# Rope's turn on VectorE, 65-to-96-token experts as two items, and the first item begun on two numbers set ahead of the list

## What is computed

```python
def rope(t, pos):                       # on q and k of the 12 dilated heads, head size 64
    t1, t2 = t[..., :32], t[..., 32:]
    return concat([t1 * cos - t2 * sin, t2 * cos + t1 * sin], -1)

# each layer
h = LN(ALPHA * h + mixer(h))            # 12 dilated (roped) + 4 forgetting heads, then w_out
probs = softmax(h @ w_router + b)       # 16 experts in 4 groups
group = argmax over groups of the sum of the two best; experts = the 2 best inside it
for e in range(16):                     # a = silu(x @ w_gate[e]) * (x @ w_up[e]); y = a @ w_down[e]
    ...
h = LN(ALPHA * h + sum of gate * y)
```

## Time and profile before

| | us |
|---|---|
| median of 3 runs | 1326.74 (1326.23 to 1327.0) |
| profiled execution | 1324.69 |
| its span, first to last instruction | 1323.0 |
| TensorE matmuls busy in it | 1114.8 (84%) |
| VectorE busy | 314.2 (24%) |
| ScalarE busy | 182.2 (14%) |
| moved by DMA | 444.7 MB, mean 336 GB/s |

### The profile page before, as it was taken

How to read it: one execution, slowest core, us unless ns; L and a number is a source line. 1 busy time by engine, 2 the same in 40 slices (tenths; PEclk the granted TensorE clock), 3 DMA queues, 4 the chain that set the end, 5 groups by cost and what they waited for, 6 DMA issues and landing times.

```text
span 1323.0 us, 16816 instructions
## 1 busy us (share of the span) xinstructions
PE 1114.8 (84%) x6068; PEld 566.8 (43%) x6069; DVE 314.2 (24%) x797; ACT 182.2 (14%) x373; POOL 4.6 (0%) x12
## 2 busy tenths in 40 slices
PE   7999988899976779777999996999998876766585
PEld 5776543344432233323677653444453332232232
DVE  0544541111111111113255363001111111111123
ACT  2233310000010000010223330100101000001000
POOL 0000000000000000000000000000000000000000
PEclk9999988899998789889899998999999987887888
DMA  9913379999999999999931434776979999999994
GB/s 377 371 64 144 138 307 428 386 429 428 428 429 429 428 428 428 428 403 424 390 128 64 174 136 192 257 261 233 430 315 377 428 428 428 428 428 429 428 404 188
DMA packets 34713, 444.70 MB, mean 336 GB/s; under 512 B 4081, under 2 KB 4337, under 8 KB 5873
## 3 DMA queue, kind: packets, MB, share of 16 engines
q1 hardware_dynamic: 33520, 439.96, 80.4%
q0 software_dynamic: 1152, 4.19, 0.8%
HBM read 443.09 MB, written 1.05 MB: 336 GB/s over the span
## 4 chain that ended last, share of the span: by engine, by line
PE 56%; DMA 36%; issue 4%; DVE 3%; ACT 0%; DVEq 0%; ACTq 0%; SPq 0%
DMA ring<-in_w_down_dram 36%; PE lo L696 10%; PE lo L589 9%; PE acc L490 9%; PE lo L601 7%; PE acc L468 5%; PE lo L576 3%; PE acc L564 3%; PE acc L654 1%; PE lo L564 1%; PE acc L542 1%; PE lo L530 1%; PE acc L736 1%; PE lo L519 1%; PE acc L763 1%
## 5 line engine op out<-in xcount | busy, mean ns | idle before, releaser
L601 PE MATMUL lo<-ring,work 128*32 128x512 f32 x2112 | 275.6, 669 | 135.0 <-DMA ring<-in_w_down_dram 124.4
L601 PEld LDWEIGHTS lo<-ring,work 128*32 128x32 f32 x2112 | 68.2, 118 | 319.2 <-issue 158.0
L589 PE MATMUL lo<-ring,work 128*64 128x512 f32 x672 | 151.9, 608 | 18.7 <-issue 13.1
L576 PEld LDWEIGHTS lo<-work,h 128*128 128x128 f32 x1088 | 131.0, 194 | 57.1 <-issue 53.5
L576 PE MATMUL lo<-work,h 128*128 128x128 f32 x1088 | 147.4, 285 | 1.9 <-DVE work L1314 1.9
L696 PE MATMUL lo<-ring,work 128*128 128x512 f32 x288 | 127.0, 601 | 11.4 <-issue 11.4
L490 PE MATMUL acc<-ring 128*128 128x256 f32 x512 | 120.9, 392 | 0.0
L490 PEld LDWEIGHTS acc<-ring 128*128 128x128 f32 x512 | 99.4, 197 | 15.5 <-issue 1.6
L589 PEld LDWEIGHTS lo<-ring,work 128*64 128x64 f32 x672 | 49.1, 140 | 116.4 <-issue 109.4
L696 PEld LDWEIGHTS lo<-ring,work 128*128 128x128 f32 x288 | 55.2, 193 | 80.3 <-issue 80.3
L1034 ACT ACTIVATE work<-lo 64x512 f32<-64x512 f32 x22 | 13.1, 594 | 468.5 <-PE lo L601 468.5
(11 more groups left out here) (191 smaller groups left out, 679.8 us busy)
## 6 DMA issues: line engine op xcount, KB each, us to landing
ring<-in_w_gate_dram SPq DMA_DIRECT2D x64, 2048.0 KB, 14.9
ring<-in_w_up_dram SPq DMA_DIRECT2D x64, 2048.0 KB, 22.6
ring<-in_w_down_dram SPq DMA_DIRECT2D x64, 2048.0 KB, 21.9
ring<-in_w_in_dram SPq DMA_DIRECT2D x24, 1024.0 KB, 26.2
ring<-in_w_out_dram SPq DMA_DIRECT2D x8, 1024.0 KB, 28.8
ln_gb<-in_ln_dram POOLq DMA_DIRECT2D x8, 512.0 KB, 11.4
cst<-in_consts_dram SPq DMA_DIRECT2D x1, 1408.0 KB, 17.6
h<-in_x_dram SPq DMA_DIRECT2D x1, 1024.0 KB, 5.3
```

The source lines that it names most:

```text
L576: mm = nc.tensor.matmul(lo[:, 2 + k // 4, (k % 4) * P:(k % 4 + 1) * P], h[:, t, k * P:(k + 1) * P], place_t[:, t], start=(k % 4 == 0 and t ...
L589: mm = nc.tensor.matmul(lo[half * W:(half + 1) * W, bank, :], lhsT, ring[:, s, at:at + 512], start=start, stop=stop, skip_group_check=True)
L601: return nc.tensor.matmul(lo[at * T:(at + 1) * T, bank, :], lhsT, ring[:, s, col:col + 512], start=start, stop=stop, skip_group_check=True)
```

## The change

Three parts.

1. `rotate` and its matrix are gone. VectorE multiplies the 32-partition quarters of q and k with a signed sin, each read from its neighbour's quarter and written to its own place; then cos, then the sum. Two waits on the rotation and one on `roped` disappear; the release of two ring slots moves from `rotate(1)` and `rotate(5)` to the first matmul of the query/key product of pairs 2 and 6.
2. The kinds grow from 3 used to 7: an expert of 65 to 96 tokens becomes a narrow item (the first 64) and a tiny one (the rest); one of 97 to 128 stays one wide item. The list is computed in another way, for up to 23 items in place of 19.
3. VectorE sets `n` and the kind of the first item ahead of the list and raises `first_ready`; TensorE waits for that between the two halves of the first gather.

```diff
-MOST = NEXP + (2 * SEQ - 1) // (P + 1)
+LIMITS = (T, W, W + T, P, P + T, P + W)
+TINY_KINDS, NARROW_KINDS, FIRST_TINY, KINDS = 3, 5, 2, 7
+FIRST_KIND = (2, 0, 1, 0, 0, 0)
+SECOND_KIND = (0, -2, 2, -1, 2, 3)
+SECONDS = (0, 1, -1, 1, 0, 0)
+MOST = NEXP + 2 * SEQ // (W + 1)
...
-                    if p < PAIRS_DIL:
-                        rotate(l, p, {1: ring_free[V_SLOT[0][1]], 5: ring_free[V_SLOT[1][1]]}.get(p))
...
-                gather(range(KB))
-                pe.wait_ge(plan_ready, l + 2)
+                gather(first_half)
+                pe.wait_ge(first_ready, l + 1)
                 n = pe.value_load(n_i[0:1, bass.ds(l, 1)], min_val=NEXP, max_val=MOST)
+                gather(second_half)
                 with pe.Fori(0, n) as j:
...
+                    pe.wait_ge(plan_ready, l + 2)
+                    pe.sem_inc(passed, 1)
...
                 v.wait_ge(qk_copied, PAIRS * l + p + 1)
-                nc.vector.tensor_tensor(dst, raw, cos, ALU.mult)
-                v.wait_ge(rot_done, PAIRS_DIL * l + p + 1)
-                step(nc.vector.tensor_tensor(part, rot, sin, ALU.mult))
-                nc.vector.tensor_tensor(dst, dst, part, ALU.add).then_inc(roped, 1)
+                for q in range(4):
+                    to, at = slice(32 * q, 32 * q + 32), slice(32 * (q ^ 1), 32 * (q ^ 1) + 32)
+                    nc.vector.tensor_tensor(turned_part[to], raw[at], sin[at], ALU.mult)
+                step(nc.vector.tensor_tensor(dst, raw, cos, ALU.mult))
+                nc.vector.tensor_tensor(dst, dst, turned_part, ALU.add).then_inc(roped, 1)
...
+                step(nc.vector.tensor_tensor(weighed, over.unsqueeze(1).to_broadcast([P, 3, NEXP, 6]),
+                                             weights.unsqueeze(2).to_broadcast([P, 3, NEXP, 6]), ALU.mult))
+                step(nc.vector.tensor_reduce(tab[:], weighed, AX.X, ALU.add))
...
+                nc.vector.tensor_scalar(kind_i[:, bass.ds(own, 1)], tab[:, 0, 0:1], float(FIRST_TINY), None, ALU.add)
+                nc.vector.tensor_copy(n_i[:, bass.ds(l, 1)], n_f[:]).then_inc(first_ready, 1)
```

More of the change, by code:

```diff
@@ L101, in constants @@
     t[:, C_COS:C_COS + SEQ] = np.cos(ang)
[L102 to L108, removed]
+    t[:, C_SIN:C_SIN + SEQ] = np.where(p % HD < 32, 1.0, -1.0)[:, None] * np.sin(ang)
+    for kind, place in enumerate((W + p % T, P + p % T, p % T, P + p % W, p % W, p, P + p)):
+        t[:, C_PLACES + kind * P:C_PLACES + (kind + 1) * P] = place + 1
     i4 = np.arange(4)
@@ L305, in build @@
         counts_done = sem("counts_done")
+        first_ready = sem("first_ready")
         plan_ready = sem("plan_ready")
@@ L491, in queries_keys @@
                                               start=(k == 0 and i == 0), stop=(k == KB - 1), skip_group_check=True)
+                        if release is not None and k == ks[0] and i == 0:
+                            mm.then_inc(release, 1)
                 if ks[-1] == KB - 1:
                     mm.then_inc(qk_done, 1)
[L495 to L505, removed]
             def scores(l, p):
@@ L894, in _ @@
                     pe.wait_ge(xg_ready, turn)
-                    with pe.If(kind < 1):
+                    with pe.If(kind < TINY_KINDS):
                         with pe.If(odd < 1):
@@ L901, in _ @@
                     with pe.Else():
-                        with pe.If(kind < 2):
+                        with pe.If(kind < NARROW_KINDS):
                             with pe.If(odd < 1):
@@ L1030, in _ @@
                     g = a.snap(start + j)
[L1031 to L1032 removed]
+                    kind = a.value_load(kind_i[0:1, bass.ds(l * ITEMS + j, 1)], min_val=0, max_val=KINDS - 1)
+                    with a.If(kind < TINY_KINDS):
                         a.wait_ge(gate_done, g + 1)
@@ L1037, in _ @@
                     with a.Else():
-                        with a.If(kind < 2):
+                        with a.If(kind < NARROW_KINDS):
                             a.wait_ge(gate_done, g + 1)
@@ L1326, in _ @@
[L1326 to L1333, removed]
@@ L1340, in _ @@
-                step(nc.vector.tensor_reduce(itab[:, 1], ended, AX.X, ALU.add))
-                step(nc.vector.scalar_tensor_tensor(out=itab[:, 2], in0=itab[:, 1], scalar=wide[:, 0:1],
-                                                    in1=iota[:, 0:ITEMS], op0=ALU.add, op1=ALU.add))
-                own = l * ITEMS
-                nc.vector.tensor_scalar(expert_i[:, bass.ds(own, ITEMS)], itab[:, 0], NEXP - 1.0, None, ALU.min)
-                nc.vector.tensor_scalar(kind_i[:, bass.ds(own, ITEMS)], itab[:, 2], -1.0, 0.0, ALU.add, ALU.max)
@@ L1374, in _ @@
                     v.sem_inc(passed, 1)
-                    with v.If(kind < 1):
+                    with v.If(kind < TINY_KINDS):
                         nc.vector.tensor_tensor(act[0:W, 0:512], lo[0:W, 0, :], silu[0:W, 0:512], ALU.mult
@@ L1383, in _ @@
                     with v.Else():
-                        with v.If(kind < 2):
+                        with v.If(kind < NARROW_KINDS):
                             nc.vector.tensor_tensor(act[:, 0:512], lo[:, 1, :], silu[:, 0:512], ALU.mult
```

103 lines of the change are left out of this document (62 added, 41 removed).

## The result

The changed kernel takes 1317.54 us (median of 5, 1315.72 to 1319.99), the one before in the same comparison 1326.23 (median of 5, 1323.66 to 1327.0): a ratio of 0.9944, 95% interval 0.9932 to 0.9955, or 7.4 us less (the two medians are 8.7 apart). The forecast was 14.3 less: right in sign and inside its range, twice too large. The profiled execution of after is the slowest of its five, 1319.99 us with a span of 1318.3. On the two traces the difference is 4.7 us (spans of 1323.0 and 1318.3).

A forecast was written before the change was run, and what follows sets the result against it. In each layer TensorE's chain sets the time first, then the weight stream at 429 GB/s. Terms -10.3 + 4.9 + 0.8 - 3.6 - 3.3 + 6.1 - 8.9 = -14.3 us give 1312.4 us, range 1301 to 1321.

The forecast's parts named there:

- The rotation: Attention: dropping the rotation's products saves TensorE 0.86 us, 12 times, -10.3 us, with rope hidden in middle iterations.
- The wait of pair 0: First scores of each layer: TensorE waits 2.45 us for rope on VectorE, +4.9 us in all.
- The clock behind the wait: Behind pair 0's wait in layer 0: it may drop to 1.2 GHz, 1.7 us; half taken, +0.8 us.
- The first item's start: Each layer's first expert item starts 1.8 us sooner through numbers set ahead of the list, -3.6 us.
- One stop for code fewer: Before layer 1's first item: a narrow form needs only the first of two code fetches, -3.3 us.
- Further stops: Layer 1's early visits to narrow code and the loop's end: one and a half more code stops, +6.1 us.
- Two items for one: Layer 1, experts 0 and 1: each wins 5.8 us as narrow plus tiny, less a 2.7 us wait; -8.9 us.
- the lighter case: Rival, 0.20: no further code stops in layer 1 (-6.1), layer 0's first item at 2.4 GHz (-2.4); 1303.9 us.
- The slower case: Rival, 0.06: VectorE's quarters cost more by moving data between partitions; decides from 1.26 us a quarter.
- The stops that were to eat the split: Rival, 0.08: three code stops near 6.2 us (18.6) in place of 6.1; 1324.9 us, no change.

The follow-up runs named there:

- e1: Kernel before the change with only the first part, rope's turn on VectorE; 1324.6 us, ratio 1.0001 to before.
- e2: Changed kernel without the split: an expert of 65 to 96 tokens is one wide item again; 1322.01 us, 0.9968 of before.
- e8: Changed kernel with the limit at 80 tokens, so in layer 1 only expert 1 is split and expert 0 is wide; 1322.29 us, 0.9979 of before.
- e4: Changed kernel with rope of pair 0 moved ahead of the forget gates' sums on VectorE; 1304.07 us, 0.9841 of before.
- e9: Changed kernel with a split expert's tiny item first and its narrow item second; 1314.25 us, 0.9916 of before.
- e7: e4 with the down matrix of expert e+1 loaded ahead of the up matrix of e+2; 1310.52 us, 0.9888 of before.
- e10: Changed kernel with both e4's early rope and e9's order of items; 1301.64 us, 0.9813 of before.
- e5: Kernel before the change with four extra unused VectorE products in rope of pair 0, making TensorE wait; 1335.28 us, 1.006 of before.

## Why the prediction was right in sign and twice too large

On the traces 4.7 us came of the 14.3 forecast. In the two attentions the gain was 0.6 and not 4.6, nearly all of that for the clock. From layer 1's first item to the gate load of expert 6 there was a loss of 1.3 where a gain of 2.8 was forecast. The two starts, with the stop that layer 1 saves, gave 5.4 and not 6.9. Against that, 1.6 came that was not in the forecast, behind layer 0's first item, whose first products run at full clock; another 1.5 was lost ahead of the first attention and behind the load of gate 6. Two groups of terms were missed by 4 us each, and it is partly luck that the medians moved by as much as half of the forecast.

- **The rotation, -10.3: right.** The middle iterations are 13.01 us apart, 13.87 before, and rope is hidden there: in a middle iteration the scores start at 85.71 without a wait, 1.4 us after rope's last instruction.
- **The wait of pair 0, +4.9: right**, 2 x 2.34. The quarters are 0.68 us each (48 of them, 678 to 687 ns) and none overlaps the one before: 2.77 for four is 0.69 each, where independent whole products lie 0.61 apart. The Trainium skill (VectorE: DVE Perf Modes, section "Two Vector instructions with no wait between them") says an instruction that starts in another quarter is held until the earlier ones are done; the trace agrees.
- **The clock behind the wait, +0.8: the step that failed.** I took half of 1.7 us. It was 4.9 (3.3 and 1.6). Waits and clock together are 9.6 of the rotation's 10.3, and e1 finds nothing left. The prediction had the mechanism and named the stretch that shows it; the size failed. It took for layer 0 a half of what one row of layer 1 lost (5.41 for 3.72), where layer 0 lost more than that on two rows (0.8 and 2.5), and for layer 1 nothing more.
- **The first item's start, -3.6: right in kind.** -1.7 in layer 0 (forecast -1.8), with TensorE waiting 0.40 us for the second item's tokens, for which the forecast had nothing. In layer 1 it was less: e2 and e8, whose first item there is wide as before, start it 14.0 and 14.4 us behind the gather, for 14.9. That the early start also carries a list 4 us longer, and so 10 us of the result, the forecast had only as a cover "costed at nothing".
- **One stop for code fewer, -3.3: right.** e2 and e8 show the gap of 8.0 us with a wide first item against 4.58. Further stops, +6.1: one came, 3.77 us behind the first narrow item, and is there in e4 as well (3.55). The other, at the first odd narrow item, did not: that item starts 0.47 us after the one before. What came instead stands behind the stop: the clock is 0.50 from 841 to 847 us, and expert 0's tiny item takes 20.9 us instead of 18.1.
- **Two items for one, -8.9: wrong.** The narrow and tiny items are nearly as long as forecast (28.0 and 17.8 us for expert 1; forecast 27.8 and 18.1). The price was not 2.7 but 7.8: expert 2 takes 25.9 us instead of 18.1. It reaches its down products 27.9 us after expert 1's second item began, not 30.1, the two halves land at 31.1 and 36.0, not by 32.8, and of the 7.8 us 5.1 are the waits and 2.5 the two groups of products between them, which take 2.95 and 3.23 us in place of 1.82 each. The other prices are the stop and the slow item behind it, 3.8 + 2.8. So experts 0 and 1 together did become shorter, 101.1 us for 105.8, and expert 2's 7.8 took more than that away.
- **Of the rivals**, the lighter case had its two halves apart: layer 0's first item does run at full clock (7.07 us for 9.50), and the load of gate 2 there issues 2.8 us earlier; but one further stop came. The slower case's condition, a quarter of 1.26 us, is far from the 0.68 measured. The stops that were to eat the split did not come: it was one and not three, and with the slow item behind it it cost 6.6 us, near the 6.1 of the forecast.

How long a first visit to code stops TensorE goes with what the transfers do meanwhile. The stops of 3.3 to 3.8 us (3.77 in after, 3.55 in e4, 3.59 in e9, 3.33 in e7) stand at a DMA share of 0.02. Those of over 6 us stand at 1.0: 6.22 and 6.91 in layer 0 of after, and also the 6.47 in layer 1 of e9, where weights still move at 433 GB/s, and the 6.03 of e10. That is a relation seen in every such stop looked at; no run changed the transfers alone.

Open remains why just this wait is followed by the lower clock. E1, e4 and e5 show that it is, not why, and layer 1 falls to the lower level at the same place without a wait too, in before and in e4. The rotation put back into the otherwise changed kernel was not tried.

## What to carry to other kernels

Work taken from the critical engine and given to an idle one is worth what its first use allows, not its average: look at the first iteration, where the receiving engine has other work ahead, and put the new work into that engine's idle time there. Here moving one call was worth nearly twice the whole change. Cost a wait on a busy array as its length and, beside it, once the instructions behind it at half clock, if any stretch of the trace shows them so. When an item is cut in two, ask which part frees the buffers and put the short one where nothing is held for it.

## What the chip showed that was not expected

A wait of 2.2 to 2.3 us, in a stretch that had been at a granted clock of 1.00, was followed by 6 to 8 us at 0.53 to 0.61 with the array never idle. Layer 0 shows it in after, e1 (0.56 from 44 to 50 us) and e5 (0.54); in before and e4, without the wait, the same stretch is at 1.00. A stop for code of 3.77 us was followed by 6 us at 0.50. Stops for code took 3.3 to 3.8 us where the DMA share was 0.02 and 6.0 to 7.2 us where it was about 1.0. And a load moved up one place in a queue of waits closed one hole of 2 us and made two of 2 and 6 us in transfers that had been full, though no byte was added: 12 us at a DMA share of 0.82, and 12 at 0.53.
